# Neighbourhood attention heads with tokens stored column by column, 2 or 3 key blocks per query block, and an earlier place for six of eight bias tables

## The reference, cut to what matters

```python
def neighbourhood_attention(q, k, v, rpb, scale):
    rows = S // GRID_W
    c = jnp.arange(GRID_W)
    c0 = jnp.clip(c - D_WIN_C // 2, 0, GRID_W - D_WIN_C)
    col_valid = (c[None, :] >= c0[:, None]) & (c[None, :] < c0[:, None] + D_WIN_C)
    ...
    def one_row(args):
        q_row, r = args
        ...
        s = jnp.einsum('bqhd,bkhd->bhqk', q_row, k_win,
                       preferred_element_type=jnp.float32) * scale
        bias = rpb_f[:, row_idx[None, :, None], col_idx[:, None, :]]
        s = jnp.where(valid, s + bias.reshape(H, GRID_W, wr * GRID_W)[None], NEG)
        p = jax.nn.softmax(s, axis=-1).astype(v.dtype)
        return jnp.einsum('bhqk,bkhd->bqhd', p, v_win)
```

## Time and profile before

| | |
|---|---|
| time, median of 3 runs | 2828.34 us (2827.85 to 2828.73) |
| the profiled execution: its own time | 2828.8 us |
| its span, first to last instruction | 2827.2 us |
| mean granted TensorE clock | 0.999 of full |
| PE busy | 2787.2 us, 99% of the span |
| PEld busy | 2059.3 us, 73% |
| DVE busy | 1674.0 us, 59% |
| ACT busy | 650.9 us, 23% |

### The profile page before, as it was taken

The page is one execution under the profiler, slowest core; times in us unless marked ns, Lnnn a source line. Parts: engine busy times, 40 slices in busy tenths (PEclk is TensorE's granted clock), DMA queues, the critical chain, the costliest instruction groups (busy, mean ns, idle before and its releaser), DMA issues.

```text
span 2827.2 us, 38717 instructions
## 1 busy us (share of the span) xinstructions
PE 2787.2 (99%) x15838; PEld 2059.3 (73%) x15838; DVE 1674.0 (59%) x3425; ACT 650.9 (23%) x1349; POOL 5.0 (0%) x22
## 2 busy tenths in 40 slices
PE   8999999999999999999999999999999999999998
PEld 3567588888644486788887557777776877788887
DVE  5685544453344874655754776766646536766654
ACT  5651311000134613211100012422221102222200
POOL 0000000000000000000000000000000000000000
PEclk9999999999999999999999999999999999999999
DMA  4013122222221132222222122211113321222222
GB/s 150 30 45 113 52 82 90 90 97 92 93 71 55 34 119 75 76 88 90 90 90 97 61 68 71 102 47 47 54 46 126 120 97 52 83 90 90 88 91 82
DMA packets 63535, 228.59 MB, mean 81 GB/s; under 512 B 7168, under 2 KB 9472, under 8 KB 62592
## 3 DMA queue, kind: packets, MB, share of 16 engines
q1 hardware_dynamic: 63360, 226.14, 23.3%
HBM read 221.91 MB, written 4.19 MB: 80 GB/s over the span
## 4 chain that ended last, share of the span: by engine, by line
PE 94%; DVE 4%; issue 1%; ACT 0%; DMA 0%; SPq 0%; DVEq 0%; ACTq 0%
PE ps L2027 30%; PE ps L726 19%; PE ps L1407 8%; PE ps L2063 8%; PE ps L1429 5%; PE ps L1804 3%; PE ps L1777 2%; PE ps L1460 2%; PE ps L1498 2%; PE ps L1789 2%; PE ps L758 1%; PE ps L2613 1%; PE ps L2634 1%; PE ps L2844 1%; PE ps L3533 1%; PE ps L1417 1%
## 5 line engine op out<-in xcount | busy, mean ns | idle before, releaser
L2027 PE MATMUL ps<-h,ring 128*128 128x256 f32 x1136 | 268.9, 379 | 2.3 <-ACT q_p L2161 2.0
L2027 PEld LDWEIGHTS ps<-h,ring 128*128 128x128 f32 x1136 | 215.0, 190 | 37.0 <-issue 7.4
L2027 PE MATMUL ps<-h_sums,w_sums 128*128 128x256 f32 x1008 | 224.4, 379 | 0.0
L2027 PEld LDWEIGHTS ps<-h_sums,w_sums 128*128 128x128 f32 x1008 | 191.5, 190 | 26.0
L726 PE MATMUL ps<-hid_sums,d_sums 128*128 128x256 f32 x740 | 175.6, 379 | 0.5 <-DVE hid_sums L1984 0.5
L726 PEld LDWEIGHTS ps<-hid_sums,d_sums 128*128 128x128 f32 x740 | 140.5, 190 | 19.9 <-issue 0.9
L1966 DVE TENSOR_TENSOR d_sums<-ring 128x512 f32<-128x512 f32 (+1 forms) x51 | 33.7, 660 | 167.8 <-DMA ring<-stream_dram 167.7
L2027 PE MATMUL ps<-c_h_sums,c_sums 128*128 128x256 f32 x504 | 112.3, 379 | 0.6 <-DVE c_sums L1972 0.6
L989 ACT ACTIVATE d_xsq<-x 128x512 f32<-128x512 f32 x47 | 28.1, 621 | 360.6 <-DVE x L950 352.3
L1789 PEld LDWEIGHTS ps<-constants,probs 128*128 128x128 f32 x560 | 62.4, 141 | 62.2 <-DVE probs L1911 47.5
L2027 PEld LDWEIGHTS ps<-c_h_sums,c_sums 128*128 128x128 f32 x504 | 95.7, 190 | 14.0 <-DVE c_sums L1972 1.0
(11 more groups left out here) (726 smaller groups left out, 5216.5 us busy)
## 6 DMA issues: line engine op xcount, KB each, us to landing
ring<-stream_dram SPq DMA_DIRECT2D x395, 512.0 KB, 3.8
bias<-bias_dram SPq DMA_DIRECT2D x8, 448.0 KB, 4.8
mem<-mem_dram SPq DMA_DIRECT2D x3, 1024.0 KB, 4.9
x_kept_dram<-x SPq DMA_DIRECT2D x1, 2048.0 KB, 10.1
x<-x_kept_dram SPq DMA_DIRECT2D x1, 2048.0 KB, 7.8
out_dram<-x SPq DMA_DIRECT2D x16, 128.0 KB, 1.9
x<-x_dram SPq DMA_DIRECT2D x3, 512.0 KB, 7.4
rope_ab<-ropes_dram SPq DMA_DIRECT2D x4, 256.0 KB, 8.4
```

What stands on the lines that cost most here:

```text
L2027: mm = pe.matmul(ps[:, bank + at, 0:256], w(k), x(k), start=start and k == 0, stop=k == 3, skip_group_check=not start)
```

## The change

- Tokens of the neighbourhood heads lie column by column (token = 8 x column + row), so a block of 128 tokens is 16 grid columns. The reordering is done in writes and reads that exist already: DVE writes `hn` through `by_columns` (steps of 8 elements) and reads the source through `by_rows`; `unnormed(4)` likewise; and the output copy reads PSUM through `by_columns` and writes `dst` in token order.
- `keys` of the neighbourhood groups is `near`: 2 key blocks for the outer query blocks, 3 for the inner ones, 10 of 16 per group. Widths are 256, 384, 384, 256.
- A bias table is 112 columns of 8 rows, again 896 wide, and the column mask has 112 elements where it had 64. The mask is now constant along the inner axis of 8 instead of being repeated along the outer one.
- `bs` has six slots. Tables 0 to 5 are prepared in steps 4, 6, 8, 10, 12 and 14, all in the latent groups, 6 and 7 in steps 24 and 26. SP loads six tables at the start and the last two once group 4's maxima are done.

```diff
-def pack_bias(rpb):
...
-    t = rpb[:, ri[:, None, :, None], ci[None, :, None, :]]
-    return np.ascontiguousarray(t.reshape(8, P, REL * GRID))
+    t = rpb[:, ri[:, None, :], ci[:, :, None]]
+    return np.ascontiguousarray(t.reshape(8, P, NEAR * GRID_H))
...
+def by_columns(t):
+    return t.rearrange("p (c r) -> p r c", r=GRID_H)
+def by_rows(t):
+    return t.rearrange("p (r c) -> p r c", c=GRID)
...
-            bs = p(f'bias{tag}', [P, 4, REL * GRID], kb + 6.5 * g * nk) if bias_heads else None
+            bs = p(f'bias{tag}', [P, BIASES, NEAR * GRID_H], kb + 6.5 * g * nk) if bias_heads else None
...
-                    m = self.c('colmask')[:, None, :].to_broadcast([P, REL, GRID])
+                    m = self.c('colmask')[:, :, None].to_broadcast([P, NEAR, GRID_H])
...
-                            a = (6 - 2 * qt) * GRID
-                            add = bs[:, gr.bias[j] % 4, a:a + w] if gr.bias else gr.mask(qt)
+                            a = NEAR_AT[qt] * GRID_H
+                            add = bs[:, gr.bias[j] % BIASES, a:a + w] if gr.bias else gr.mask(qt)
...
-                    if i + 2 < n and units[i + 2][1] in (0, 1) and groups[units[i + 2][0]].bias:
-                        shape_bias(units[i + 2][0], units[i + 2][1])
+                    if bias_heads and 4 <= i < 4 + 2 * BIASES and i % 2 == 0:
+                        shape_bias((i - 4) // 2)
+                    if bias_heads and n - 8 <= i < n - 4 and i % 2 == 0:
+                        shape_bias(BIASES + (i - n + 8) // 2)
...
-                            ins = dve.tensor_copy(dst, ps[:, at, :])
+                            if groups[p].columns:
+                                ins = dve.tensor_copy(dst.rearrange("p (r c) -> p r c", c=GRID), by_columns(ps[:, at, :]))
+                            else:
+                                ins = dve.tensor_copy(dst, ps[:, at, :])
...
                 for h in bias_heads:
-                    if h >= 4:
-                        p = next(n for n, gr in enumerate(groups) if h - 4 in (gr.bias or ()))
+                    if 4 <= h < BIASES:
+                        sync.wait_ge(*s[f'biasin{h % 4}'].at(16))
+                    if h >= BIASES:
+                        p = next(n for n, gr in enumerate(groups) if h - BIASES in (gr.bias or ()))
                         sync.wait_ge(*s['maxed'].at(4 * (p + 1)))
...
+        near = lambda qt: (max(0, qt - 1), min(4, qt + 2))
...
                        + [group([qd[r, i, :] for r in rows], [kd[r, i, :] for r in rows], vd, 4 + i, 64 ** -0.5,
-                                bias=(2 * i, 2 * i + 1)) for i in range(4)])
+                                near, bias=(2 * i, 2 * i + 1), columns=True) for i in range(4)])
...
-                self.scale_tiles(dve, self.tiles(self.x), lambda i: self.v('g_mix', DT + i), hn, self.root[:, :])
+                self.scale_tiles(dve, [by_rows(t) for t in self.tiles(self.x)], lambda i: self.v('g_mix', DT + i),
+                                 [by_columns(t) for t in hn], by_rows(self.root[:, :]))
...
-                unnormed(4, qd[:, 0, :])
+                dve.wait_ge(*s['l_p'].at(5))
+                dve.tensor_tensor(by_columns(qd[:, 0, :]), by_rows(ps[:, 0, :]), by_rows(self.root[:, :]),
+                                  ALU.mult).then_inc(*s['l_out'].up())
```

More of the change, by code:

```diff
@@ L35 @@
 WIN_C = 16
-REL = 14
+GRID_H = S // GRID
+NEAR = 112
+BIASES = 6
+NEAR_AT = 0, 32, 32, 80
 UNIT_BLOCKS = 8
@@ L265, in pack_bias, with near_columns @@
 def pack_bias(rpb):
-    c = np.arange(GRID)
-    ci = np.clip(c[None, :] - c[:, None] + WIN_C - 1, 0, 2 * WIN_C - 2)
-    ri = np.arange(REL)[None, :] + 1 - np.arange(2)[:, None]
-    t = rpb[:, ri[:, None, :, None], ci[None, :, None, :]]
-    return np.ascontiguousarray(t.reshape(8, P, REL * GRID))
+    at = np.arange(P)
+    ci = np.clip(near_columns()[1][None, :] - at[:, None] // GRID_H + WIN_C - 1, 0, 2 * WIN_C - 2)
+    ri = np.arange(GRID_H)[None, :] - at[:, None] % GRID_H + GRID_H - 1
+    t = rpb[:, ri[:, None, :], ci[:, :, None]]
+    return np.ascontiguousarray(t.reshape(8, P, NEAR * GRID_H))
+def near_columns():
+    tile = np.repeat(np.arange(3), (32, 48, 32))
+    return np.array([0, 1, GRID // 16 - 1])[tile], np.concatenate([seq(0, 32), seq(-16, 48), seq(-16, 32)])
 def pack_s5(a):
@@ L293, in pack_s5 @@
     return small, np.ascontiguousarray(big)
-CONSTS = [('ident', P), ('ones', P), ('ones64', P), ('band', 3 * P), ('colmask', GRID),
+CONSTS = [('ident', P), ('ones', P), ('ones64', P), ('band', 3 * P), ('colmask', NEAR),
           ('carry', S), ('before', CH), ('upto', CH), ('eye', CH), ('level', 6 * CH)]
@@ L318, in constants @@
     z['band'] = np.where(np.abs(j[None, :] - P - i[:, None]) <= P, 0.0, NEG)
[L319 to L322, removed]
+    tile, k = near_columns()
+    c0 = np.clip(16 * tile[None, :] + i[:, None] // GRID_H - WIN_C // 2, 0, GRID - WIN_C)
+    k = 16 * tile[None, :] + k[None, :]
+    z['colmask'] = np.where((k >= c0) & (k < c0 + WIN_C), 0.0, NEG)
     z['carry'] = np.tile(np.where(np.arange(S) % CH == 0, 0.0, 1.0), (P, 1))
@@ L1277 @@
     sink: Any = None
+    columns: bool = False
     folded: bool = False
@@ L1731, in attention @@
             sb = p(f'shaped{tag}', [P, 2, g, nk * P], kb + 5.5 * g * nk) if any(shaped) else None
-            bs = p(f'bias{tag}', [P, 4, REL * GRID], kb + 6.5 * g * nk) if bias_heads else None
-            st = p(f'stats{tag}', [P, 4, 6, 2], kb + 6.5 * g * nk + (14 if bias_heads else 0))
+            bs = p(f'bias{tag}', [P, BIASES, NEAR * GRID_H], kb + 6.5 * g * nk) if bias_heads else None
+            st = p(f'stats{tag}', [P, 4, 6, 2], kb + 6.5 * g * nk + (3.5 * BIASES if bias_heads else 0))
             ns = p(f'sinks{tag}', [P, 8], kb + 6.5 * g * nk + 0.5) if groups[-1].sink is not None else None
@@ L1867, in _, with shape_bias @@
                     dve.tensor_scalar(ns[:, 2 * i:2 * i + 2], sink, -1.0, None, ALU.mult).then_inc(*s['copied'].up())
-                def shape_bias(p, j):
-                    h = groups[p].bias[j]
+                def shape_bias(h):
                     dve.wait_ge(*s[f'biasin{h % 4}'].at(16 * (h // 4 + 1)))
-                    v = bs[:, h % 4, :].rearrange("p (a b) -> p a b", b=GRID)
-                    m = self.c('colmask')[:, None, :].to_broadcast([P, REL, GRID])
-                    dve.scalar_tensor_tensor(out=v, in0=v, scalar=1.0 / groups[p].scale, in1=m, op0=ALU.mult,
+                    v = bs[:, h % BIASES, :].rearrange("p (a b) -> p a b", b=GRID_H)
+                    m = self.c('colmask')[:, :, None].to_broadcast([P, NEAR, GRID_H])
+                    dve.scalar_tensor_tensor(out=v, in0=v, scalar=1.0 / groups[-1].scale, in1=m, op0=ALU.mult,
                                              op1=ALU.add).then_inc(*s['vec'].up())
@@ L1943, in _ @@
                 for h in bias_heads:
[L1944 to L1945 removed]
+                    if 4 <= h < BIASES:
+                        sync.wait_ge(*s[f'biasin{h % 4}'].at(16))
+                    if h >= BIASES:
+                        p = next(n for n, gr in enumerate(groups) if h - BIASES in (gr.bias or ()))
                         sync.wait_ge(*s['maxed'].at(4 * (p + 1)))
[L1947 removed]
+                    sync.dma_start(bs[:, h % BIASES, :], self.bias_d[h]).then_inc(*s[f'biasin{h % 4}'].up(16))
                 self.prefetch(sync)
@@ L2534, in mixer_cd, with group @@
         out = [q[:, 2 * i, :] for i in range(4)] + self.tiles(qd)
-        def group(q, k, v, i, scale, **kw):
+        near = lambda qt: (max(0, qt - 1), min(4, qt + 2))
+        def group(q, k, v, i, scale, keys=lambda qt: (0, 4), **kw):
             return HeadGroup([[t] for t in q], [[t] for t in k], lambda b, j: [v[:, b, P * (i % 4) + 64 * j:P * (i % 4) + 64 * j + 64]],
-                             [[(6, 64 * j, 64)] for j in range(2)], [(6, out[i])], scale, keys=lambda qt: (0, 4), **kw)
+                             [[(6, 64 * j, 64)] for j in range(2)], [(6, out[i])], scale, keys=keys, **kw)
         groups = ([group([q[:, 2 * i + j, :] for j in range(2)], [k[:, 2 * i + j, :] for j in range(2)], v, i, 96 ** -0.5)
```

1 line of the change is left out of this document (removed).

## The result

| | before | after |
|---|---|---|
| time, median | 2828.27 us (2827.85 to 2828.73) | 2813.77 us (2813.49 to 2814.49) |
| span of the profiled execution | 2827.2 us | 2812.3 us |
| PE busy | 2787.2 us | 2771.3 us |
| DVE busy | 1674.0 us | 1667.0 us |
| mean granted TensorE clock | 0.999 | 0.999 |

Four runs of each, on the same chip. The ratio is 0.9949, with a 95% interval of 0.9936 to 0.9963. The gain is 14.5 us where 13.0 were predicted.

What follows compares the result with a forecast made beforehand. PE was taken as the bound, holding 94% of the chain. Narrow units 15.9 us, less 0.8, 1.2 and 0.9 for tables and copies, gave 13.0 us: 2828.34 to 2815.3 us, range 2813.5 to 2819.2.

Steps and rivals of the forecast that it cites:

- the sink's column: Extra in the window mixer's banded heads, absent from the neighbourhood heads: one more exponential column and a small POOL copy; given nothing.
- copies: Output copies reading in steps of 8 elements: 0.7 us for steps 25 and 29, 0.2 for the seventh group, sum 0.9.
- The stretch: PE's time from the first neighbourhood score on `k_d` to the first non-fill `Down` product: 63.07 us before, 49.3 predicted.
- tables 6 and 7: Bias tables on DVE in steps 24 and 26: 0.2 and 1.0 us passed on to PE, together 1.2 us.
- narrow units, by the banded yardstick: Neighbourhood stretch should match the window mixer's banded heads of the same widths: 63.07 to 47.17, 15.90 us gained.
- table in step 4: Bias table in a latent step where no values run yet: PE's transpose waits, costing 0.8 us.
- eight tiles: DVE's tiles of `hn` in steps of 8 elements: 2.9 us more, hidden under 3.4 us of cover before PE needs them.
- The wait of step 27: PE's wait before the transpose of that step, predicted at about 1.5 to 1.9 us.
- The table of step 14: Existing latent unit with a table: 3.48 us on DVE under PE's 3.79 period, so tables in steps 6 to 14 cost nothing.
- Rival 2: The tables don't hide: each of six costs its 1.0 us, 6.0 for 0.8; gain 7.8, time 2820.5 us; chance 0.06.
- Rival 1: Small steps are dear: 0.72 us extra per instruction on tiles and copies; gain 9.6, time 2818.7 us; chance 0.17.
- Rival 3: Strided accesses much dearer, passing the gain at 1.55 us each; at 2.0, time 2833.7 us; chance 0.05.

## Why the prediction was right, step by step

The mechanism held: PE's narrower work brought the gain, and the tables cost what was forecast (0.80 for 0.8, 1.14 for 1.2). Two terms of the sum were off, and both the same way: the sink's column, given nothing, was worth 0.6 us, and the copies, charged with 0.9, cost nothing. Together they are the 1.5 us between 13.0 and 14.5. The stretch was predicted at 49.3 us and took 47.69. With the prediction's own 1.2 for tables 6 and 7, the sink's 0.61 taken off the yardstick and the copies at 0, it would have been 47.17 - 0.61 + 1.2 = 47.76. That the result still fell inside the range, by 0.3 us, owes something to luck: the lower end of 2813.5 stands lower than the 2814.4 that the prediction reached with its copies at 0, and it named no term for the rest.

| term | predicted, us | measured, us | shown by |
|---|---|---|---|
| narrow units, by the banded yardstick | -15.9 | -16.5 | the stretch with no sink column, 46.55 |
| table in step 4 | 0.8 | 0.80 | its wait, which goes with tables from step 6 on |
| tables 0 to 5 otherwise | 0 | 0 | period 3.80 us |
| tables 6 and 7 | 1.2 | 1.14 | the remainder 47.69 - 46.55; seven slots take away 1.0 of it |
| copies | 0.9 | 0 | 688 ns; 0.89 when they write in steps instead |
| eight tiles | 2.9, hidden | 2.5, hidden | 7.86 against 5.38; PE's step at 759.95 |
| sum | -13.0 | -14.6 | |

Two rows of the kernel before bear on the first term: the custom instruction on a bias table, and the one with the sink's column. The prediction did not compare them.

```profile
L1893 DVE CUSTOM_DVE_ANT_0 shaped<-ps,bias 128x512 f32<-128x512 f32 x32 | 20.8, 688 | 5.5 <-PE ps L1777 5.3
...
L1893 DVE CUSTOM_DVE_ANT_0 shaped<-ps,constants,sinks 128x256 f32<-128x256 f32 x16 | 7.1, 481 | 2.6 <-PE ps L1777 2.6
```

- **Narrow units** was the right term by the right yardstick, with one difference named and given nothing: the sink. It costs 60 ns for each of 32 custom instructions, and 0.61 us of it had reached PE. The trace of the kernel before held this price, in the two rows above. On a bias table the instruction takes as long as plain maxima of its width (688 against 686 ns); with the sink it takes 59 ns more than they do (481 against 422). And even without a size the difference had a sign: work that the yardstick has and the changed stretch lacks can only make it too long.
- **Copies** was the mis-sized term that mattered most. I sized reads of PSUM, reads of SBUF and writes of SBUF alike from L1620, whose operand lies in SBUF. The price fits SBUF (358 ns for one stepping source, 386 for the destination, against the 360 that I took) and not PSUM, where it is nothing. My lower end of 0 held this case, and with it the prediction would have been 2814.4. One more flaw lies in the 0.36 itself: the contiguous reductions that it was set against read PSUM and L1620 reads SBUF.
- **The wait of step 27** was expected at 1.5 to 1.9 us and is 1.24. Its lower end was 0.56 + 1.0. Of the missing 0.3, the sink's column explains 0.12: with a constant start the banded wait at this place is 0.44 instead of 0.56. The rest is not shown by a run; step 24's table makes PE wait 0.17 before (949.67), and time that PE has lost there it need not wait here. The copy mattered less than I thought: dearer by 350 ns, it lengthens this wait only to 1.35.
- **The table of step 14** as a model for the other latent steps was exact. 3.48 us of DVE work under 3.79 of PE's hid it in every step, three in a row as well. Rival 2 falls.
- **Rival 1** falls too. A tile takes 1129 ns, 0.39 us more than the contiguous 743; the 1.46 us (0.743 + 0.72) of that rival is not reached. Back to back the eight cost 2.5 us more, 0.31 each, where 0.36 was taken. By the Trainium skill, page "Vector Engine (DVE) Microarchitecture Reference", section 5.2 "Measured stream behaviour on trn2", small steps on the destination cost about 2.5 ns an element (its case is 24 words). Steps of 8 here come to 743 + 386 ns for 512 elements, an extra of 0.75 ns each: nearer to its figure for far hops. The measurement decides; no run here has steps of 24.
- **Rival 3** needed 1.55 us for each access. The dearest one seen, two stepping sources, costs 0.59.
- **The loads** showed nothing: 4.9 us to land, and no wait of DVE on a bias table.

The opening's 0.4 us belongs to no term; it differs from execution to execution of the same kernel.

What stays open: how the 1.14 us divides between tables 6 and 7 (1.01 is measured for the one of step 26; no run has narrow units and no late table at all); and how the price of a step in SBUF depends on its length between 2 (nothing on a write) and 8 elements. No run has a step between. Nor is it shown why two stepping sources cost more than one.

## What to carry to other kernels

Take as a yardstick a stretch of the same trace that already has the shapes you are going to, then list what that stretch has and the new one lacks, with a sign even where you have no size. Before a small operation is moved, compare the other engine's time for that step with and without it: work that costs little in a long step (0.7 us for all the tables here) costs several times as much once the steps are made shorter (2.4 to 2.8), so the two edits belong together. If an access has to go in steps and a copy out of PSUM exists anyway, let it be that copy's read, which cost nothing here.

## What the runs showed of the hardware

All on DVE, in 32-bit elements; 512 of them in each partition where no other number stands:

- A copy that reads PSUM in steps of 8 or 64 elements takes 688 and 687 ns, and 688 when it reads contiguously (the kernel before): the steps cost nothing.
- In SBUF, writing in steps of 8 costs 386 ns (743 to 1129), writing in steps of 64 costs 350 (688 to 1038), one source in steps of 64 costs 358 (743 to 1101), and two sources 587 (743 to 1330). The tile of `qd`, which writes in steps of 8 what it computes from PSUM and `root`, goes from 691 to 1093. These are durations of single instructions; back to back, eight tiles cost 0.31 us each more for the write and 0.36 and 0.58 for one and two sources. The same section of the Trainium skill has 1.73 ns an element for one source that hops 4 KiB every element and 1.76 for two, about the same. Here, with steps of 256 bytes, the second source adds 229 ns, 0.45 ns an element, so for these steps the trace disagrees on that point.
- The custom add-and-maximum takes 60 ns more when its start value is a column in SBUF instead of a constant, at 256 (421 to 480) and at 384 elements (554 to 614) alike.
- A second source that is constant along its inner axis is free: the bias tables, 896 elements, take 1086 ns with such a mask, and took 1.08 us with one that repeats along the outer axis.
